# Five places of a three-block network: gated recurrence on its own banks, copies of transposes ahead of activations, a pipelined spatial gate, and two norms summed in other ways

## What is computed

```python
# first block: a layer norm after the feed-forward part, and one inside the convolution branch
x = layer_norm(DN_ALPHA * x + 0.5 * swiglu_ffn(x, ...), ln1_g[i], ln1_b[i])
c = causal_depthwise_conv(c, conv_dw_w) + conv_dw_b        # 31 taps
c = jax.nn.silu(layer_norm(c, conv_ln_g, conv_ln_b))
# second block: a state space branch (convolution of 5 taps, silu, chunked scan) and, on the
# other half of the width, a gated linear recurrence: forget gates f = sigmoid(h @ W_f), state
# S_t = f_t * S_(t-1) + (1 - f_t) v_t^T, output q_t^T S_t, in both directions, then an output matrix
# third block: a spatial gate, one 128x128 matrix over the tokens of each chunk per group of channels
```

## Time and profile before

| | us |
|---|---|
| median of 3 runs | 4484.01 |
| the profiled execution, its own time | 4483.24 |
| its span | 4481.4 |
| TensorE busy | 4331.1 (97%) |
| VectorE busy | 2717.4 (61%) |
| ScalarE busy | 793.4 (18%) |
| GpSimd busy | 171.5 (4%) |

### The profile page before, as it was taken

The page is one execution under the profiler, slowest core; times in us unless marked ns, Lnnn a source line. Parts: engine busy times, 40 slices in busy tenths (PEclk is TensorE's granted clock), DMA queues, the critical chain, the costliest instruction groups (busy, mean ns, idle before and its releaser), DMA issues.

```text
span 4481.4 us, 68176 instructions
## 1 busy us (share of the span) xinstructions
PE 4331.1 (97%) x29692; PEld 3361.7 (75%) x29692; DVE 2717.4 (61%) x4765; ACT 793.4 (18%) x1434; POOL 171.5 (4%) x281
## 2 busy tenths in 40 slices
PE   9999999999999999999999999999999998999899
PEld 7887445577887888876755678887888787777767
DVE  6675878355555446676444556566556548888736
ACT  0001012221022000221222210000100104444311
POOL 0000000010000000000000000000000003222100
PEclk9999999999999999999999999999999999999999
DMA  7533454103222222111210122222222210000031
GB/s 256 169 115 64 68 75 69 29 2 85 94 94 66 94 85 87 59 57 38 66 48 29 55 69 93 85 85 76 94 73 88 81 47 12 2 3 3 12 103 48
DMA packets 284378, 311.52 MB, mean 70 GB/s; under 512 B 5168, under 2 KB 277936, under 8 KB 281008
## 3 DMA queue, kind: packets, MB, share of 16 engines
q1 hardware_dynamic: 284080, 307.16, 24.2%
HBM read 305.04 MB, written 2.10 MB: 69 GB/s over the span
## 4 chain that ended last, share of the span: by engine, by line
PE 90%; DVE 6%; ACT 2%; issue 1%; DMA 0%; SPq 0%; DVEq 0%; POOL 0%; ACTq 0%; POOLq 0%
PE ps L399 50%; PE ps L323 18%; PE ps L368 2%; PE ps L3459 1%; PE ps L2703 1%; PE ps L2489 1%; PE ps L938 1%; PE ps L923 1%; PE ps L954 1%; PE ps L540 1%; PE ps L2169 1%; PE ps L2158 1%; PE ps L3362 1%; PE ps L1383 1%; PE ps L754 0%
## 5 line engine op out<-in xcount | busy, mean ns | idle before, releaser
L399 PE MATMUL ps<-main 128*128 128x256 f32 x5888 | 1305.7, 379 | 0.0
L399 PEld LDWEIGHTS ps<-main 128*128 128x128 f32 x5888 | 1119.8, 190 | 151.0
L399 PE MATMUL ps<-main,w 128*128 128x256 f32 x4436 | 992.7, 380 | 3.5 <-DVE main L472 1.8
L399 PEld LDWEIGHTS ps<-main,w 128*128 128x128 f32 x4436 | 844.4, 191 | 122.9 <-issue 7.5
L323 PE MATMUL ps<-main,w 128*128 128x512 f32 (+1 forms) x1952 | 843.6, 587 | 12.7 <-DMA main<-in_xT 7.6
L323 PEld LDWEIGHTS ps<-main,w 128*128 128x128 f32 x1952 | 370.0, 193 | 423.7 <-issue 409.7
L491 DVE TENSOR_TENSOR main<-main,ps 128x512 f32<-128x512 f32 x189 | 130.0, 688 | 455.3 <-PE ps L399 454.9
L488 DVE TENSOR_TENSOR main<-main,ps 128x512 f32<-128x512 f32 x123 | 84.4, 686 | 233.8 <-PE ps L399 231.0
L438 ACT COPY main<-ps 128x256 f32<-128x256 f32 x123 | 45.7, 371 | 964.8 <-PE ps L399 962.4
L764 DVE SCALAR_TENSOR_TENSOR main<-main,params_sb 128x512 f32<-128x512 f32 x256 | 192.5, 752 | 9.1
L496 DVE TENSOR_TENSOR main<-main,ps 128x512 f32<-128x512 f32 x189 | 130.0, 688 | 86.9 <-PE ps L399 84.4
(11 more groups left out here) (512 smaller groups left out, 4824.6 us busy)
## 6 DMA issues: line engine op xcount, KB each, us to landing
w<-in_w_in SPq DMA_DIRECT2D x58, 1024.0 KB, 8.1
w<-in_e_w_in SPq DMA_DIRECT2D x28, 1024.0 KB, 5.1
main<-in_ada_w SPq DMA_DIRECT2D x24, 1024.0 KB, 5.0
w<-in_ffn_wu SPq DMA_DIRECT2D x22, 1024.0 KB, 6.3
w<-in_ffn_wg SPq DMA_DIRECT2D x21, 1024.0 KB, 6.4
w<-in_o_w_in SPq DMA_DIRECT2D x20, 1024.0 KB, 5.5
w<-in_ffn_wd SPq DMA_DIRECT2D x16, 1024.0 KB, 5.1
w<-in_w_up SPq DMA_DIRECT2D x16, 1024.0 KB, 5.3
```

The source lines that it names most:

```text
L399: t = pe.mm(PS[b][:, 256 * half:256 * half + 256], weight[:, m, :], x(m), start=m == 0, stop=m == n - 1)
```

## The change

1. **ln1** joins `DIRECT` with four squares. The `mod` products around it are split 14, mean, 16, columns, 9, spread, 9 (before 14, 24, 5, 5).
2. **Convolution norm:** VectorE adds the eight convolved tiles, into the room of the first padded input `Cp(0)`: six adds behind the convolution of tile 6, the seventh two steps on. `pe_ln` takes the one total.
3. **State space branch:** ScalarE copies transposes of the first chunks before the last two activations. On TensorE the first piece of the query projection stands before the first scores, not behind.
4. **Gated recurrence:** forget gates use banks 2 and 3 alone, the output tile bank 2, everything of the levels banks 4 to 7 (before all of 2 to 7). The output tile is cut into 3, 3 and 2 products, and VectorE reads it one step later.
5. **Spatial gate:** two tiles are transposed ahead of the last seven-product step before it, and then each next tile two ahead of its product.

```diff
 def dve_total(v, name, k, X, ready):
-            v.tt(t512[5], t512[5] if k > 1 else X(0), X(k), ADD)...
+            T = Cp(0)[:, 0:TOK] if name == "conv ln" else t512[5]
+            v.tt(T, T if k > 1 else X(0), X(k), ADD)...
-    DIRECT = {"ln3": 4, "ln4": 4, "b2 in": 3}
+    DIRECT = {"ln1": 4, "ln3": 4, "ln4": 4, "b2 in": 3}
 def pe_ln(...)
-            pe_sum(pe, ("mean", name), [X(k) for k in range(8)], [(*ready, k) for k in range(8)])
+        pe_sum(pe, ("mean", name), [t512[5] if total is None else total], [("total", name, 7)])
 pe_mixers
-        pe_ln(pe, "conv ln", Yc, ("conv31",), between, lambda pe: some(more, 1))
+        pe_ln(pe, "conv ln", Cp(0)[:, 0:TOK], between, lambda pe: some(more, 1))
 dve_mixers
             if f in (0, 2, 4, 5):
                 conv31((4, 0, 5, 0, 6, 7)[f])
+            for k in {4: range(1, 7), 6: (7,)}.get(f, ()):
+                dve_total(v, "conv ln", k, Yc, ("conv31",))
 pe_ssd
+                if not n and not d:
+                    next(more, None)
                 b, before = banks.take("ssd sc", d, c)
...
-                next(more, None)
+                if n or d:
+                    next(more, None)
 act_ssd
-        for f in range(12):
+        for f in range(10):
...
+            convolved(f)
         for c in range(NT):
...
+            if c > 1:
+                convolved(8 + c)
 gated recurrence
-    G_hf = [Gemm(f"hf{d}", w_in2, 3600 + 1024 * d, 8, 8, H, h2) for d in range(2)]
+    G_hf = [Gemm(f"hf{d}", w_in2, 3600 + 1024 * d, 8, 8, H, h2, among=(2, 3)) for d in range(2)]
-        b, before = banks.take(g.name, f)
+        b, before = banks.take(g.name, f, among=(2,))
-            if k == 3:
+            if k in (2, 5):
                 yield
 dve_hg_fill
-        for _ in range(5):
+        for _ in range(6):
             yield
 pe_hgrn
-        banks.only(range(2, 8))
+        banks.only(range(4, 8))
 pe_even
-        for step in steps[3:18]:
+        for step in steps[3:17]:
             run(pe_seven(pe, *step))
+        for f in range(2):
+            turned_gate(f)
+        run(pe_seven(pe, *steps[17]))
         for f in range(8):
...
+            if f < 6:
+                turned_gate(f + 2)
 tensor_program
-        pe_ln(pe, "ln1", between=lambda pe: some(mod, 24), late=lambda pe: some(mod, 5))
+        pe_ln(pe, "ln1", between=lambda pe: some(mod, 16), late=lambda pe: some(mod, 9))
```

More of the change, by code:

```diff
@@ L547, in dve_total @@
         if k:
-            v.tt(t512[5], t512[5] if k > 1 else X(0), X(k), ADD).then_inc(v.inc(sem["dve", "norm"], "total", name, k), 1)
+            T = Cp(0)[:, 0:TOK] if name == "conv ln" else t512[5]
+            v.tt(T, T if k > 1 else X(0), X(k), ADD).then_inc(v.inc(sem["dve", "norm"], "total", name, k), 1)
     def dve_direct_total(v, name, k):
@@ L662, in dve_rstd, with pe_ln @@
         return out
[L664 to L667, removed]
-            pe_sum(pe, ("mean", name), [X(k) for k in range(8)], [(*ready, k) for k in range(8)])
+    def pe_ln(pe, name, total=None, between=lambda pe: None, late=lambda pe: None):
+        pe_sum(pe, ("mean", name), [t512[5] if total is None else total], [("total", name, 7)])
         between(pe)
@@ L2220, in act_ssd, with convolved @@
             act_softplus(a, s, ("ssd dt", d), s_dt[d], s_tmp)
-        for f in range(12):
-            if f % 2 == 0 and 0 < f < 10:
-                act_seven(a, G_xbc, f + 2)
+        def convolved(f):
             V, k = conv5(f)
@@ L2226, in act_ssd @@
             a.act(V(k), t512[f % 4], ACT.Silu, bias=par("conv_b_2", f)).then_inc(a.inc(s, "xbc", f), 1)
+        for f in range(10):
+            if f % 2 == 0 and 0 < f < 10:
+                act_seven(a, G_xbc, f + 2)
+            convolved(f)
         for c in range(NT):
@@ L2854, in pe_even, with turned_gate @@
         run(more)
-        for step in steps[3:18]:
-            run(pe_seven(pe, *step))
-        for f in range(8):
+        def turned_gate(f):
             b, before = banks.take("sgu tp", f)
@@ L2864, in pe_even @@
             t.then_inc(pe.inc(s, "mm", "sgu tp", f), 1)
+        for step in steps[3:17]:
+            run(pe_seven(pe, *step))
+        for f in range(2):
+            turned_gate(f)
+        run(pe_seven(pe, *steps[17]))
+        for f in range(8):
             b, before = banks.take("sgu", f)
@@ L2892, in silu, with turned_gate @@
             a.act(U3.ap, U3.ap, ACT.Silu).then_inc(a.inc(s, "out", g.name, j), 1)
-        for g, j, kg in steps[3:18]:
+        def turned_gate(f):
+            a.wait_ge(*at("mm", "sgu tp", f))
+            a.copy(t512[f], bank("sgu tp", f)).then_inc(a.inc(s, "out", "sgu tp", f), 1)
+        for n, (g, j, kg) in enumerate(steps[3:18], 3):
+            if n == 17:
+                for f in range(2):
+                    turned_gate(f)
             act_seven(a, g, j)
@@ L2896, in act_even @@
                 silu(g, j)
-        for f in range(8):
-            a.wait_ge(*at("mm", "sgu tp", f))
-            a.copy(t512[f], bank("sgu tp", f)).then_inc(a.inc(s, "out", "sgu tp", f), 1)
+        for f in range(2, 8):
+            turned_gate(f)
         for g, j, kg in steps[18:26]:
```

## The result

The changed kernel takes **4447.14 us** (median of 4 runs, 4440.27 to 4447.96), the kernel before, in the same comparison, 4482.16 (4 runs, 4474.57 to 4486.97). The ratio is 0.992, with a 95% interval of 0.9903 to 0.9938: 0.8% faster, or 35.0 us. The prediction was 4444.5, in a range of 4436 to 4458. The profiled execution is 4447.25 us long, its span 4445.2.

The account below looks back on a forecast made before the run. TensorE, busy 97% of the span and 90% of the last-ending chain, was taken as the bound. Gains of 0.6 + 6.0 + 7.2 + 18.1 + 7.6 = 39.5 us from 4484.0 gave 4444.5 us, range 4436 to 4458.

Parts of the forecast that it names:

- The cover: Convolution norm: VectorE's 4.8 us of added sums stay hidden behind other work, with 3.5 us of cover left.
- A fall of the clock inside costs nothing up to 2.3 us: State space start: DVE is late next and TensorE waits 2.3 us for it, so a clock fall hides there.
- Both mechanisms: Gated recurrence: own forget-gate banks end six 1.17 us waits; the 3+3+2 cut covers eight 1.39 us waits before the transposes.
- Rival (b): Gated recurrence: DVE or ACT truly bounds the rounds, so the 11.1 us returns one wait later; 4455.6 us, chance 0.11.
- Rival (d): Gated recurrence: with four banks each level waits for DVE, 7 x 8 x 1.17 = 65.5 us; slower, 4510 us, chance 0.02.
- the 2.9 us lead: Gated recurrence: DVE's pick frees the next state product's bank 2.9 us before TensorE takes it, the tightest take.
- The one new wait: Spatial gate: the fifth product takes the first one's bank and waits 0.95 us for DVE to read it.
- Rival (e): Whole kernel: the change gives nothing because a later stage waits for something that does not move; 4484 us, chance 0.03.
- so I take the fall: 2.3 - 1.7 = 0.6: First norm: 2.3 us gained at full clock, less 1.7 us for one fall to half clock, leaves 0.6 us.
- -1.1 with two: First norm: lower bound of the gain, a loss of 1.1 us if the clock falls twice.
- Rival (a): First norm: the clock stays full because TensorE is no longer idle, gaining 2.3 us, not 0.6; 4442.8 us, chance 0.12.
- Rival (c): Clock falls at three new places (pipelined gate, behind the DVE wait at 1980, a round), 3 x 1.7 us; 4449.6, chance 0.11.

Follow-up runs that it names:

- ln1_wide: The changed kernel with the first norm's column products writing 128 equal columns instead of one; first norm 19.30 us, 4442.73 us in all, ratio 0.991.
- no_ln1: The changed kernel with the first norm as it was before the change; first norm 21.34 us, 4442.90 us in all, ratio 0.991.
- after_again: The changed kernel once more, unaltered, against the kernel before; 4442.93 us (5 runs), ratio 0.9908.

## Why the prediction was right, and where it was not

The time lies 2.6 us from the forecast, and the sum of the five terms is right to 1.3 us, in part by luck: the first norm came out 2.9 us worse than forecast, and three other terms 0.2 to 0.7 us better.

**Convolution norm, 6.0 predicted, 6.01 measured**, and 6.01 when undone. The count of records times their spacing was all of it. The cover held: TensorE's wait behind it stayed at 1.83 us.

**State space start, 7.2 against 7.84.** The step, with DVE as the one that is late next, is right: its row releases L2172.

```profile
1971.64 3.70 PE L2161 MATMUL ps<-main,consts_sb 128*128 128x512 f32 x8 [0.96 <-DVE main L2335]
...
1978.92 1.22 DVE L2347 TENSOR_TENSOR main<-main 128x1024 f32<-128x1024 f32 x1
...
1980.28 1.97 PE L2172 MATMUL ps<-main 128*128 128x64 f32 x16 [1.50 <-DVE main L2347]
```

L2172 was put at 1980.05 and came at 1980.28, in a trace whose stage began 0.90 us later (1961.21): DVE's row of work was 0.6 to 0.7 us shorter than worked out. The 2.3 us that TensorE was to wait for DVE are 0.96 and 1.50, in two places. "A fall of the clock inside costs nothing up to 2.3 us" was too generous: with the piece in its old place a fall that made it 1.4 us longer, behind a 2.99 us stop, went with 2.2 us more in the stretch; how much of that the fall alone costs was not tried.

**Gated recurrence, 18.1 against 18.80.** Both mechanisms and both prices held apart from each other (7.0 and 11.3). By the waits the sum is 11.1 + 7.0 + 0.8 (a level behind L2475, not foreseen) less 1.1 (the first level's wait, which grew, not foreseen either), 17.8; 1.0 us I cannot place. Rival (b) fell with the same rows: the 11.1 us did not come back one wait later. Rival (d), the four banks that cost more than they give, fell as its condition said: the 2.9 us lead was there (DVE's pick L2563 ends at 2274.20, the next L2616 starts at 2277.16). Halving the banks once more used it up, and then the wait was 2.63 us once a round. Rival (d)'s price, every level of every round, was the wrong count even there.

**Spatial gate, 7.6 against 7.79**, and 7.80 when undone. The one new wait was put at 0.95 us and is 1.12. Rival (e) fell with the whole: 35.0 us are gone from the time.

**First norm, 0.6 predicted, 2.28 lost.** The step that failed is "so I take the fall: 2.3 - 1.7 = 0.6": one fall was taken for 40 one-column records, from a row with 24 of them. TensorE's work at full clock is 2.3 us shorter, to a tenth (ln1_wide). But the falls cost 4.6 us in the first trace, 3.0 in most others and 1.6 in one (20.93). So with one-column products this part gains nothing: its usual 22.27 us stand against 21.61 before and 21.34 in no_ln1, whose whole time, 4442.90, is that of the changed kernel in after_again, 4442.93. The bound "-1.1 with two" did not even hold the first of these. Rival (a) had it right that this part is worth 2.3 us with a full clock, and wrong about what keeps it full. The rule that it leaned on, activity releases the throttle (the Trainium skill, same page, section "What's actually happening"), does not cover this: PE is busy for 5.00 of 5.00 us at 0.54, and full at 1.00 with the same records and 128 columns.

**The clock elsewhere.** The forecast let every stretch outside the change keep its time. They add up to +1.96 us in the first trace, of which +5.09 in the projections. Rival (c), three new falls worth 5 us, came near the sum by another way: in the projections the falls stand at the old places, and their number varies; the pipelined gate, the place behind the DVE wait at 1980 and the rounds have none that is new. The five places gave 38.2 us of the 39.5 worked out; the medians of the two comparisons differ by 35.0 and by 39.4 (4482.31, the kernel before in its other eight runs, less 4442.93), one on either side of it.

## What to carry to other kernels

Price a change by records and waits at full clock, then ask separately where TensorE issues products with few output columns: being busy is not enough to keep the clock. Where a column of sums is all that is wanted and the free columns of the bank are there, 128 equal columns cost the same time as one here; that the whole kernel gains by it is not shown (4440.43 and 4440.60 against 4447.14 and 4442.93, with overlapping intervals). Count how often a shortage of banks is met from the take with the smallest lead, not from the number of takes, and don't give cover to a step that stands behind a stop of 2 to 3 us at its full-clock price.

## What the hardware showed that was not expected

- One-column float32 products take as long as 128-column ones at full clock (24 records in 2.73 us and in 2.84), and in these two stretches the half clock came in every trace with one-column products (ten of the first norm, twelve of the projections), though TensorE stopped for at most 0.94 us at a time, and in none of the two each with 128. What exactly the chip measures stays open: widths between were not tried here. The 64-column products of the rounds, put between 512-column ones, leave the clock at 1.00 (2270 to 2520).
- The same program varies by 3.4 us in one stretch through this alone (325.16 and 321.79), in steps of about 1.7.
- A stop of 1.83 us ahead of 40 small products left the clock alone in nine traces and lowered it in three (6.36 us for the 40 records in place of 4.73); one of 2.79 us lowered it both times.
